# A mixture-of-experts encoder layer on one core: expert results stored in token order by indirect DMA, and read back with plain transfers

## What is computed

```python
h = rmsnorm(x, norm_ffn_g)
g_sel = argmax(h @ w_grp + b_grp)                  # one of 4 groups
top_v, top_i = top_k(exp_logits_of_that_group, 2)  # two of its 8 experts
expert_id = g_sel[:, None] * 8 + top_i
for e in range(32):
    hid = silu(h @ w_gate[e]) * (h @ w_up[e])      # 1024 -> 512
    y = y + combine[:, e:e + 1] * (hid @ w_down[e])  # 512 -> 1024
return rmsnorm(x + y, final_norm_g)
```

## Time and profile before

| | |
|---|---|
| median of three executions | 861.25 us |
| span of the profiled execution | 857.0 us (its own time outside the profiler is not given; the span runs from its first to its last instruction) |
| TensorE busy | 763.1 us (89%) |
| VectorE, ScalarE, GpSimd busy | 224.5, 163.3, 63.6 us |
| moved by DMA | 238.90 MB, 279 GB/s over the span |
| mean granted clock of TensorE | 0.972 |

### The profile page before, as it was taken

One profiled execution on the slowest core, in us unless ns is written; L12 is line 12 of the kernel. 1 busy time (PEld: TensorE's weight loads), 2 busy tenths in 40 slices (PEclk: granted clock), 3 DMA queues, 4 the chain that ended last, 5 costly groups with the idle time before them and its releaser, 6 DMA issues.

```text
span 857.0 us, 14144 instructions
## 1 busy us (share of the span) xinstructions
PE 763.1 (89%) x6112; PEld 378.4 (44%) x6112; DVE 224.5 (26%) x429; ACT 163.3 (19%) x315; POOL 63.6 (7%) x49
## 2 busy tenths in 40 slices
PE   6997999999999997799999999999999988988830
PEld 3443444464566555444444444444444334334310
DVE  3037544003355257411111111111111101111116
ACT  5244120014344254201010101010101000000004
POOL 0714000000000034100000000000000000000023
PEclk9999999999999998899999999999999999999975
DMA  9322020402450362499999999999999999999945
GB/s 330 77 98 98 1 99 1 148 1 81 177 216 2 117 275 99 169 395 417 420 420 416 420 419 418 420 418 418 419 417 420 419 417 421 418 418 420 416 169 227
DMA packets 54011, 238.90 MB, mean 279 GB/s; under 512 B 5856, under 2 KB 7264, under 8 KB 37600
## 3 DMA queue, kind: packets, MB, share of 16 engines
q1 hardware_dynamic: 47712, 225.93, 65.5%
q10 hardware_dynamic: 5120, 8.39, 2.6%
q0 software_dynamic: 1152, 4.19, 1.4%
HBM read 228.02 MB, written 10.49 MB: 278 GB/s over the span
## 4 chain that ended last, share of the span: by engine, by line
PE 58%; SPq 16%; DMA 14%; DVE 6%; ACT 3%; issue 2%; POOL 1%; POOLq 0%; ACTq 0%; DVEq 0%
PE bank L408 17%; SPq L321 13%; PE bank L700 13%; DMA arena<-in_w_up 9%; PE bank L719 7%; PE bank L690 6%; PE bank L569 4%; DMA arena<-in_w_down 3%; PE bank L620 3%; DVE arena L998 2%; SPq L332 2%; PE bank L603 2%; PE bank L511 1%; DMA arena<-rows_out,arena 1%; PE bank L587 1%
## 5 line engine op out<-in xcount | busy, mean ns | idle before, releaser
L700 PE MATMUL bank<-arena 128*64 128x512 f32 x1024 | 227.9, 594 | 14.0 <-DMA arena<-in_w_up 13.2
L408 PE MATMUL bank<-arena 128*128 128x512 f32 x384 | 171.0, 601 | 5.9 <-ACT arena L799 5.9
L700 PEld LDWEIGHTS bank<-arena 128*64 128x64 f32 x1024 | 73.5, 137 | 162.4 <-issue 137.7
L719 PE MATMUL bank<-arena 128*64 128x512 f32 x512 | 116.9, 598 | 15.7 <-ACT arena L952 15.1
L408 PEld LDWEIGHTS bank<-arena 128*128 128x128 f32 x384 | 72.2, 191 | 94.5 <-issue 90.5
L690 PEld LDWEIGHTS bank<-arena 128*128 128x128 bf16 x3072 | 92.3, 98 | 25.2 <-issue 25.2
L690 PE MATMUL bank<-arena 128*128 128x64 bf16 x3072 | 96.0, 194 | 0.0
L998 DVE TENSOR_TENSOR arena<-bank,arena 128x256 f32<-128x256 f32 (+1 forms) x80 | 30.3, 395 | 249.3 <-ACT arena L948 214.1
L719 PEld LDWEIGHTS bank<-arena 128*64 128x64 f32 x512 | 34.5, 136 | 77.6 <-issue 62.1
L948 ACT ACTIVATE arena<-bank 128x256 f32<-128x256 f32 x32 | 12.3, 384 | 284.8 <-PE bank L700 284.8
L1273 DVE COPY arena<-bank 128x512 f32<-128x512 f32 x32 | 22.1, 692 | 120.7 <-PE bank L719 120.7
(11 more groups left out here) (157 smaller groups left out, 506.0 us busy)
## 6 DMA issues: line engine op xcount, KB each, us to landing
arena<-in_w_gate SPq DMA_DIRECT2D x64, 1024.0 KB, 23.3
arena<-in_w_up SPq DMA_DIRECT2D x64, 1024.0 KB, 23.1
arena<-in_w_down SPq DMA_DIRECT2D x32, 2048.0 KB, 26.1
arena<-in_w_in SPq DMA_DIRECT2D x6, 2048.0 KB, 8.1
rows_out<-arena ACTq DMA_DIRECT2D x64, 128.0 KB, 6.1
arena<-in_x SPq DMA_DIRECT2D x4, 512.0 KB, 5.9
arena<-in_w_out SPq DMA_DIRECT2D x2, 1024.0 KB, 8.0
arena<-in_w_out SPq DMA_DIRECT2D x1, 2048.0 KB, 18.3
```

Source lines behind the costliest of these rows:

```text
L408: m = pe.matmul(pbank[n % UNIT_BANKS][:], lhs(k), rhs(k), start=(k == 0), stop=(k == KC - 1))
L700: mm = pe.matmul(pbank[s][64 * half:64 * half + 64, :].rearrange("p (g f) -> p g f", g=2), xT[:, k], wg_sb[s][:, :, k, half * 256:(half + ...
L719: mm = pe.matmul(pbank[5 + s][64 * half:64 * half + 64, :], hidT[:, kc % 2, kc // 2], wd_sb[s][:, kc, half * 512:(half + 1) * 512], start= ...
```

## The change

The experts' results go to a DRAM tensor in token order, `y_tok`, with two planes of 512 tokens: plane 0 for a token's lower-numbered expert, plane 1 for the higher-numbered one; each token has two rows of 2 KB. For that a table is built after the routing: VectorE works out each token's destination rows, GpSimd scatters them by slot into the DRAM tensor `slot_tok` (which SP has filled with a number out of bounds, 2048), reads the table back twice (once for each half of the partitions), adds 1 for the upper half and makes integers of it. In the loop GpSimd, instead of ScalarE, stores an expert's `y_sb` with one indirect DMA of 128 rows; rows whose destination is out of bounds, the empty slots, are skipped. At the end SP reads plane 0 when expert 30 is stored, and plane 1 when expert 31 is, each in four plain transfers of 512 KB. VectorE adds plane 0 to `x1` for all four tiles, then plane 1, with weights re-ordered by plane (`comb_by`). The arena grows by 1 KB per partition, and the DMA scratch is set to 8192.

```diff
@@ -65,14 +65,15 @@
 def mixer_and_moe(nc, x, rpb, w_in, w_g2, b_g, gla_g, g_mix, w_out, g_ffn, g_ffn_T, w_r, b_r, w_gate, w_up, w_down, g_fin,
-                  c_small, c_mask, c_scan, out, limit=SLOTS):
+                  c_small, c_mask, c_scan, c_tok, out, limit=SLOTS):
     with ExitStack() as ctx:
-        arena = ctx.enter_context(nc.sbuf_tensor("arena", [P, words(207)], F32))
+        arena = ctx.enter_context(nc.sbuf_tensor("arena", [P, words(208)], F32))
         pbank = [ctx.enter_context(nc.psum_tensor(f"bank{i}", [P, 512], F32)) for i in range(8)]
...
         both_b = ctx.enter_context(nc.sbuf_tensor("both_b", [P, TT, EXPERTS], BF16))
-        rows_out = nc.dram_tensor("rows_out", [EXPERTS * SLOTS, D], F32).ap()
+        y_tok = nc.dram_tensor("y_tok", [2 * T * 2, D // 2], F32).ap()
+        slot_tok = nc.dram_tensor("slot_tok", [SLOTS * EXPERTS, 1], F32).ap()
@@ -199,10 +200,21 @@
         wd_sb = [at(48 * i + 32, FC, D) for i in range(RING)]
-        got = [[at(4 * (2 * t + k), D) for k in range(2)] for t in range(TT)]
+        got = [at(96, TT, D), at(112, TT, D)]
         res = at(32, TT, D)
-        x2 = at(96, TT, D)
-        junk3 = at(112, TT, D)
+        x2 = x1
+        junk3 = at(0, TT, D)
+
+
+        extra = at(207, 256)
+        tab_f, tab_u = extra[:, 0:32], extra[:, 32:64].bitcast(U32)
+        tok_c = extra[:, 64:64 + 2 * TT + 1]
+        tok_lo, tok_hi, half_col = tok_c[:, 0:TT].unsqueeze(2), tok_c[:, TT:2 * TT].unsqueeze(2), tok_c[:, 2 * TT:]
+        later = extra[:, 80:84].unsqueeze(2)
+        sooner = extra[:, 84:88].unsqueeze(2)
+        dest = extra[:, 88:96].rearrange("p (t k) -> p t k", k=2)
+        comb_by = extra[:, 96:104].rearrange("p (t k) -> p t k", k=2)
+        part = extra[:, 104:112].rearrange("p (t k) -> p t k", k=2)
@@ -255,7 +267,8 @@
                                                             sem("d_done"), sem("y_evicted"))
-        gathered = [[sem(f"gathered{t}_{k}") for k in range(2)] for t in range(TT)]
+        sooner_in, later_in = sem("sooner_in"), [sem(f"later_in{t}") for t in range(TT)]
+        tab_step, tab_blank, tab_in, tab_written = sem("tab_step"), sem("tab_blank"), sem("tab_in"), sem("tab_written")
         x2_half, x2_done, sumsq3_done, ms3_done = sem("x2_half"), sem("x2_done"), sem("sumsq3_done"), sem("ms3_done")
@@ -273,7 +286,8 @@
         wd_d = w_down.rearrange("l e (k p) d -> (l e) p k d", p=P)
-        rows_out_d = rows_out.rearrange("(e t) (h d) -> e h t d", t=SLOTS, h=2)
+        y_tok_d = y_tok.rearrange("(k t p h) d -> k t p (h d)", k=2, t=TT, h=2)
+        slot_tok_d = slot_tok.rearrange("(s e) o -> s (e o)", e=EXPERTS)
@@ -304,6 +318,9 @@
             sp.dma_start(b_r_sb, b_r.broadcast_to((P, GROUPS + EXPERTS))).then_inc(late_in, 16)
+            sp.dma_start(tok_c, c_tok).then_inc(late_in, 16)
+            sp.wait_ge(tab_step, 1)
+            sp.dma_start(slot_tok_d, tab_f[0:SLOTS]).then_inc(tab_blank, 16)
             for g in range(3, 7):
@@ -367,6 +384,11 @@
             sp.dma_start(gfb, g_fin.broadcast_to((P, D))).then_inc(gf_in, 16)
+            for k in range(2):
+                for s in range(RING):
+                    sp.wait_ge(y_stored[s], 16 * len(range(s, EXPERTS - 1 + k, RING)))
+                for t in range(TT):
+                    sp.dma_start(got[k][:, t], y_tok_d[k, t]).then_inc(later_in[t] if k else sooner_in, 16)
             sp.wait_ge(most_done, 1)
@@ -385,6 +407,9 @@
             sp.wait_ge(out_stored, 16 * TT)
+            sp.wait_ge(sooner_in, 16 * TT)
+            for t in range(TT):
+                sp.wait_ge(later_in[t], 16)
@@ -951,20 +976,13 @@
-            def rows_store(e, c, s):
-                act.wait_ge(y_evicted, c + 1)
-                for half in range(2):
-                    act.dma_start(rows_out_d[e, half], y_sb[s][64 * half:64 * half + 64]).then_inc(y_stored[s], 16)
-
             with act.Fori(0, (EXPERTS - 2) // RING) as i:
...
                     hidden_T_evict(s, RING * i + s)
-                    rows_store(RING * i + s, RING * i + s, s)
             for e in (EXPERTS - 2, EXPERTS - 1):
...
                 hidden_T_evict(e % RING, e)
-                rows_store(e, e, e % RING)
@@ -1014,7 +1032,7 @@
             dve.wait_ge(g_done, 1)
-            dve.wait_ge(late_in, 48)
+            dve.wait_ge(late_in, 64)
             for m in range(4):
@@ -1246,7 +1264,11 @@
                     then(nc.vector.tensor_reduce(rank[:, :, k:k + 1], prod, AX.X, ALU.add))
-                then(nc.vector.scalar_tensor_tensor(slotf, eid, float(SLOTS), rank, ALU.mult, ALU.add))
+                then(nc.vector.scalar_tensor_tensor(slotf, rank, float(EXPERTS), eid, ALU.mult, ALU.add))
+                tt(later, eid[:, :, 0:1], eid[:, :, 1:2], ALU.is_gt)
+                then(tt(sooner, eid[:, :, 0:1], eid[:, :, 1:2], ALU.is_lt))
+                nc.vector.scalar_tensor_tensor(dest[:, :, 0:1], later, float(2 * T), tok_lo, ALU.mult, ALU.add)
+                then(nc.vector.scalar_tensor_tensor(dest[:, :, 1:2], later, float(-2 * T), tok_hi, ALU.mult, ALU.add))
                 nc.vector.tensor_copy(slot, slotf).then_inc(slots_done, 1)
@@ -1256,6 +1278,10 @@
                 then(tt(comb[:, :, 1:2], comb[:, :, 0:1], eexp, ALU.mult))
+                tt(part, comb, later.broadcast_to((P, TT, 2)), ALU.mult)
+                then(tt(comb_by, comb, sooner.broadcast_to((P, TT, 2)), ALU.mult))
+                tt(comb_by[:, :, 0:1], comb_by[:, :, 0:1], part[:, :, 1:2], ALU.add)
+                then(tt(comb_by[:, :, 1:2], comb_by[:, :, 1:2], part[:, :, 0:1], ALU.add))
@@ -1269,7 +1295,7 @@
                 if stored is not None:
-                    dve.wait_ge(y_stored[s], 32 * stored)
+                    dve.wait_ge(y_stored[s], 16 * stored)
                 nc.vector.tensor_copy(y_sb[s], pbank[5 + s][:]).then_inc(y_evicted, 1)
@@ -1319,7 +1345,7 @@
                                                    ALU.add).then_inc(a_cw, 1)
-                nc.vector.tensor_copy(x2, x1).then_inc(a_acc, 1)
+                nc.vector.tensor_copy(x2[:, 0, 0:1], x2[:, 0, 0:1]).then_inc(a_acc, 1)
                 dve.wait_ge(a_cw, 2 * TT)
@@ -1340,13 +1366,14 @@
             with dve.If(general < limit + 1):
+                dve.wait_ge(sooner_in, 16 * TT)
                 for t in range(TT):
-                    dve.wait_ge(gathered[t][0], 16)
-                    nc.vector.scalar_tensor_tensor(x2[:, t], got[t][0], comb[:, t, 0:1], x1[:, t], ALU.mult,
+                    nc.vector.scalar_tensor_tensor(got[0][:, t], got[0][:, t], comb_by[:, t, 0:1], x1[:, t], ALU.mult,
                                                    ALU.add).then_inc(x2_half, 1)
+                for t in range(TT):
                     dve.wait_ge(x2_half, t + 1)
-                    dve.wait_ge(gathered[t][1], 16)
-                    nc.vector.scalar_tensor_tensor(x2[:, t], got[t][1], comb[:, t, 1:2], x2[:, t], ALU.mult,
+                    dve.wait_ge(later_in[t], 16)
+                    nc.vector.scalar_tensor_tensor(x2[:, t], got[1][:, t], comb_by[:, t, 1:2], got[0][:, t], ALU.mult,
                                                    ALU.add).then_inc(x2_done, 1)
@@ -1355,7 +1382,7 @@
         def _(pool):
-
+            nc.gpsimd.memset(tab_f, float(EXPERTS * SLOTS)).then_inc(tab_step, 1)
             pool.wait_ge(bias_in, 16 * NA_HEADS + 16)
@@ -1388,17 +1415,26 @@
+            last_row = EXPERTS * SLOTS - 1
             pool.wait_ge(slots_done, 1)
-            for s in range(RING):
-                pool.wait_ge(y_stored[s], 32 * len(range(s, EXPERTS, RING)))
-            pool.wait_ge(most_done, 1)
-            general = pool.value_load(most[0:1, 0:1], min_val=0, max_val=T)
-            with pool.If(general < limit + 1):
-                for t in range(TT):
-                    for k in range(2):
-                        nc.gpsimd.indirect_dma_start(got[t][k], None, rows_out,
-                                                     bass.IndirectOffsetOnAxis(ap=slot[:, t, k:k + 1], axis=0)
-                                                     ).then_inc(gathered[t][k], 16)
+            pool.wait_ge(tab_blank, 16)
+            for t in range(TT):
+                for k in range(2):
+                    nc.gpsimd.indirect_dma_start(slot_tok, bass.IndirectOffsetOnAxis(ap=slot[:, t, k:k + 1], axis=0),
+                                                 dest[:, t, k:k + 1], None, bounds_check=last_row,
+                                                 oob_is_err=False).then_inc(tab_written, 16)
+            pool.wait_ge(tab_written, 16 * 2 * TT)
+            for half in range(2):
+                pool.dma_start(tab_f[64 * half:64 * half + 64], slot_tok_d).then_inc(tab_in, 16)
+            pool.wait_ge(tab_in, 32)
+            nc.gpsimd.tensor_tensor(tab_f, tab_f, half_col.broadcast_to((P, EXPERTS)), ALU.add).then_inc(tab_step, 1)
+            pool.wait_ge(tab_step, 2)
+            nc.gpsimd.tensor_copy(tab_u, tab_f).then_inc(tab_step, 1)
```

(17 more changed lines are left out.)

## The result

The changed kernel takes 853.25 us (median of 4 executions, 852.03 to 854.42), against 861.67 us for the kernel before in the same comparison (861.05 to 863.12): a ratio of 0.990, 95% interval 0.989 to 0.992. That is 8.4 us faster. Forecast were 847.4 us, about 14 us faster; the range, 841.5 to 854.5, holds the result.

What follows compares the result with a forecast made beforehand. The DMA engines were taken to bound the expert loop, a chain of latencies the end. From 861.25 us, 4.9 (stores 5.9 less table 1.0) and 9.0 for the end came off: 847.4 us, range 841.5 to 854.5.

Steps and rivals of the forecast that it cites:

- The stores in the loop: Saturated expert loop: storing only filled rows saves 5.9 us, between bounds of 0 and 9.8 us.
- even relief: Rival, expert loop: all DMA engines relieved alike, 9.8 us less 1.0 for the table; 843.5 us, chance 0.21.
- layout in fours: Loop stores: rows laid out in fours of neighbouring partitions; the lowest engine keeps 179 of 248 rows, saving 5.9 us.
- The table: Eight scatters and read back from about 358 us: cost 1.0 us of DMA time in the loop, 0 to 5 kept.
- The end: After the last down projection: early reads and a smaller last scatter shorten the end by 9.0 us, from 34.0 to 25.0.
- D: End of the last down projection, 823.05 us in the kernel before; the end of the kernel is counted from it.
- The walk of 17.1 us: Kernel's end: old durations followed from the first closing sum to the end of the span, 17.1 us, where it was 21.2.
- write-port case: Last scatter: GpSimd cannot write descriptors during certain VectorE copies; 0 expected with VectorE idle, an estimated 2.5 us if hit.
- No relief in the loop: Rival, expert loop: busiest engine keeps its rows or skipped rows are moved all the same; 853.3 to 854.9 us, chance 0.15.
- the other signs: Signs of a wrong forecast: under 415 GB/s in the loop, VectorE waiting for an output buffer, last scatter over 5 us.
- slower: Rival, saturated loop: indirect writes fall on few engines; 876.2 us, chance 0.08.
- late end: Rival, kernel's end: the last scatter is slow, so the end gains 5.7 us; 850.7 us, chance 0.11.

Runs made afterwards that it cites:

- fixed_full: fixed_low, but all 64 slots of every expert, empty ones too, stored through the indirect path; 851.1 us, ratio 0.987 to the kernel before.
- fixed_low: Changed kernel without the table: fixed destinations, the reference's number of filled slots per expert, at the lowest slots; 844.87 us, ratio 0.981 to the kernel before.
- early_slots: Changed kernel with slots and destinations worked out before the first rows' eviction, scatters starting at 354.78 instead of 358.55; 851.8 us, ratio 0.989 to the kernel before.

## Why the prediction was right, and where it was not

**The direction and the path.** Right: faster, by a relief of the saturated stream and by a shorter end, and both were there. The size was not: 14 us forecast, 8.4 measured, for one step, the table.

**The stores in the loop: 5.9 us.** Right in size, in part by luck. The loop shrank by 6.5 (6.6 without the table), and the working's two assumptions held in direction: skipped rows cost nothing (fixed_full gives the gain back), and rows at the lowest slots bring less than spread ones. But the even relief was put 1.4 us too high (9.8; the even layout brings 8.4) and the penalty for the lowest slots 2.1 too high (9.8 - 5.9 = 3.9 by the layout in fours; measured 1.8), and the two errors nearly cancel. The Trainium skill, "DMA: Bandwidth & Descriptors", section The descriptor swizzle, states such fours for a transfer of 128 partitions. By that rule the trace agrees in sign, with the 1.8 us and with the loads that finish further apart in fixed_low; no row names a packet's engine.

**The table: 1.0 us, bounds 0 to 5.** This step failed. It cost 8.4 us, beyond its bound. I priced its bytes and packets in the stream, and its latency against the use of the buffer (ready by 385, which held: GpSimd's conversion ends at 385.2). "GpSimd has nothing else to do there" was true and beside the point. What was missing is that eight indirect transfers issued back to back stall TensorE: no row of the kernel before shows that, since its own eight gathers come when TensorE is done. The bound should have been open above, at the 10 us for which the scatters run, since no row excluded a coupling while they do.

**The end: 9.0 us.** The mechanism was right, the size 0.9 too large. The first closing sum was put at D + 7.9, bound by the first sums; their last ends at 827.77 + 4.87 = 832.64, D + 7.5, and the bound was the last plane instead. Its three terms were each somewhat longer: the scatter starts 1.5 us after D instead of 0.8 (GpSimd takes 0.71 us of "issue" after its wait), lands in 4.0 instead of 3.6, and the read takes 3.2 instead of 2.8. The walk of 17.1 us held. GpSimd's issue took 0.97 us beside an idle VectorE, so the write-port case weighed in the prediction did not arise.

**The sum.** 14.9 us of gain were seen as 6.5 + 8.1 = 14.6 in the two stretches, and 8.6 were lost between them. "No relief in the loop" gave 853.3 to 854.9, where the time came out to within 0.1 us, and the text named as its sign that the last expert would be as late as it was. It was, at 825.18; yet that rival is false. The range reached to 854.5 for its sake alone, so that it holds the time is luck. A sign made of a sum (the place of the last expert) could not tell a missing gain from a gain with a loss beside it; the length of the loop from expert 1 could. Of the other signs, the stream kept 418 GB/s over the loop and VectorE waited for no output buffer.

The cases *slower* and *even relief* fall; *late end* too, since the last scatter landed in 4.0 us.

## What to carry to other kernels

When a run of indirect DMAs goes beside a busy TensorE, look whether TensorE keeps its pace: a block of matmuls broken up by idle time labelled "issue" while the run lasts is the sign. Letting each one land before the next removes most of the cost, and making the indices with small matmuls in an existing wait removes all that shows. Where a stream bounds a loop, price in what delays the release of its buffers, not only bytes; a hole in the stream is lost for good. Measure a loop from a mark inside it to a mark inside it, so that a gain and a loss do not hide each other.

## What the runs showed that was not expected

- Eight indirect scatters, 1.29 us apart, cost 6.7 to 9.2 us wherever they stood in the loop; 6 to 8 us apart, each after the landing of the last, they cost 2.7 together.
- In early_slots the signal of a matmul recorded until 356.39 arrived at 361.89. Engines that wait for TensorE then look stalled themselves, VectorE for 8.0 us.
- Rows skipped for being out of bounds appear on the software queue as tiny packets (four bytes a row) and leave the price per MB stored as it was, 2.6 us of all engines against 2.5.
- Scattered rows of four bytes slow other transfers while they run (234 GB/s at a share of 1.16), rows of 512 bytes do not (418 at 1.02); the time lost at that place is the same.
- A dip of the granted clock followed TensorE's stall: 0.50 from 368 to 376 us, and a down projection of 5.18 us instead of 3.65.
